# Token-major x and y in a three-stage transformer layer: wide down and output products, roots per token

## The reference

```python
def rmsnorm(x, g):
    y = x * lax.rsqrt(jnp.mean(x * x, axis=-1, keepdims=True) + EPS)
    return y * g
def adaln_in(x, g, shift, scale):
    return rmsnorm(x, g) * (1 + scale) + shift
def swiglu(h, wg, wu, wd):
    return (jax.nn.silu(h @ wg) * (h @ wu)) @ wd
def trunk_layer(x, mod, p, ml_state, ssm_state, n_seg):
    h = adaln_in(x, g[0], sh(0), sh(1))
    x = x + 0.5 * sh(2) * rmsnorm(swiglu(h, p['w_gate'][0], p['w_up'][0], p['w_down'][0]), g[1])
    h = adaln_in(x, g[2], sh(3), sh(4))
    mix, new_ml, new_ssm = hybrid_mixer(h, p, ml_state, ssm_state, n_seg)
    x = x + sh(5) * rmsnorm(mix, g[3])
    h = adaln_in(x, g[4], sh(6), sh(7))
    x = x + 0.5 * sh(8) * rmsnorm(swiglu(h, p['w_gate'][1], p['w_up'][1], p['w_down'][1]), g[5])
```

## Time and profile before

| | us |
|---|---|
| median of 3 executions | 3079.03 |
| lowest and highest of them | 3078.14, 3079.24 |
| the profiled execution, span from first to last instruction | 3079.0 |
| PE busy | 3027.0 (98%) |
| POOL busy | 1825.1 (59%) |
| DVE busy | 1352.3 (44%) |
| ACT busy | 974.9 (32%) |
| mean granted TensorE clock, as a share of full speed | 0.993 |

### The profile page before, as it was taken

One profiled execution on the slowest core, in us unless ns is written; L12 is line 12 of the kernel. 1 busy time (PEld: TensorE's weight loads), 2 busy tenths in 40 slices (PEclk: granted clock), 3 DMA queues, 4 the chain that ended last, 5 costly groups with the idle time before them and its releaser, 6 DMA issues.

```text
span 3079.0 us, 48036 instructions
## 1 busy us (share of the span) xinstructions
PE 3027.0 (98%) x17401; PEld 2859.1 (93%) x17401; DVE 1352.3 (44%) x2931; ACT 974.9 (32%) x1226; POOL 1825.1 (59%) x906
## 2 busy tenths in 40 slices
PE   6999999999999999999999999999999999999998
PEld 2899999999999998899999999899999999999998
DVE  3365566556655665876733352522343111100113
ACT  2322322232222223534332233523222322222223
POOL 2565665566556555557754545566565666566666
PEclk8999999999999999999999999999999999999999
DMA  9866675667566756655444435246554644444443
GB/s 363 280 219 197 220 225 177 206 211 232 175 207 205 232 183 199 220 161 157 138 135 128 118 106 171 73 128 190 168 179 139 143 149 129 126 126 126 126 129 109
DMA packets 494159, 531.54 MB, mean 173 GB/s; under 512 B 29275, under 2 KB 454723, under 8 KB 493123
## 3 DMA queue, kind: packets, MB, share of 16 engines
q1 hardware_dynamic: 458048, 508.62, 52.4%
q10 hardware_dynamic: 35971, 21.27, 2.5%
HBM read 519.12 MB, written 9.66 MB: 172 GB/s over the span
## 4 chain that ended last, share of the span: by engine, by line
PE 91%; DVE 2%; POOL 2%; issue 2%; DMA 1%; ACT 1%; ACTq 1%; DVEq 0%; POOLq 0%
PE banks L784 25%; PE banks L786 25%; PE banks L785 25%; PE banks L959 4%; PE banks L960 4%; PE banks L961 4%; DVE HB L2261 1%; PE banks L870 1%; POOL w_lo L2557 1%; PE banks L813 1%; PE banks L1275 0%; PE banks L1295 0%; DMA w_raw<-in_ffn_w_gate_dram 0%; ACTq L1503 0%; PE banks L1280 0%
## 5 line engine op out<-in xcount | busy, mean ns | idle before, releaser
L2557 POOL TENSOR_TENSOR w_lo<-w_raw,w_hi 128x1024 fp32r<-128x1024 f32 (+1 forms) x668 | 1595.8, 2395 | 1033.0 <-ACT w_hi L1378 1032.5
L784 PE MATMUL banks<-xn_hi,w_hi 128*128 128x384 f32 x3920 | 1329.9, 339 | 5.2 <-POOL w_lo L2557 2.1
L786 PE MATMUL banks<-xn_hi,w_lo 128*128 128x384 f32 x3920 | 1311.7, 335 | 0.0
L785 PE MATMUL banks<-xn_lo,w_hi 128*128 128x384 f32 x3920 | 1311.6, 335 | 0.0
L1378 ACT ACTIVATE w_hi<-w_raw 128x1024 fp32r<-128x1024 f32 (+1 forms) x668 | 704.2, 1057 | 1463.5 <-PE banks L786 743.8
L784 PEld LDWEIGHTS banks<-xn_hi,w_hi 128*128 128x128 f32 x3920 | 737.4, 188 | 29.4 <-issue 22.4
L785 PEld LDWEIGHTS banks<-xn_lo,w_hi 128*128 128x128 f32 x3920 | 737.4, 188 | 4.2 <-issue 3.1
L786 PEld LDWEIGHTS banks<-xn_hi,w_lo 128*128 128x128 f32 x3920 | 736.9, 188 | 0.0
L1876 DVE SCALAR_TENSOR_TENSOR banks<-w_raw,cT,banks 128x256 f32<-128x256 f32 x1372 | 548.0, 483 | 0.0
L1989 DVE TENSOR_TENSOR AM<-AM,banks 128x384 f32<-128x384 f32 x88 | 44.8, 551 | 598.1 <-PE banks L786 598.1
L784 PE MATMUL banks<-hid_hi,w_hi 128*128 128x384 f32 x704 | 235.2, 334 | 0.0
(11 more groups left out here) (293 smaller groups left out, 1819.5 us busy)
## 6 DMA issues: line engine op xcount, KB each, us to landing
w_raw<-in_w_ada_dram SPq DMA_DIRECT2D x288, 512.0 KB, 5.5
w_raw<-in_ffn_w_gate_dram SPq DMA_DIRECT2D x176, 512.0 KB, 4.4
w_raw<-in_ffn_w_up_dram SPq DMA_DIRECT2D x176, 512.0 KB, 3.9
w_raw<-in_ffn_w_down_dram SPq DMA_DIRECT2D x176, 512.0 KB, 3.7
w_raw<-in_w_in_dram SPq DMA_DIRECT2D x104, 512.0 KB, 3.7
w_raw<-in_w_out_dram SPq DMA_DIRECT2D x32, 512.0 KB, 3.5
HB<-row_wait ACTq DMA_DIRECT2D x12, 512.0 KB, 4.7
x_wait<-xT ACTq DMA_DIRECT2D x1, 3072.0 KB, 9.9
```

Of the source, the lines that this page charges most:

```text
L784: pe.matmul(out, wh, hi, start=start, stop=False)
L785: pe.matmul(out, wh, lo, start=False, stop=False)
L786: return pe.matmul(out, w_lo[:, w, off:off + P], hi, start=False, stop=stop)
L2557: pool.tensor_tensor(used(w_lo[:, slot(p), :], p), used(w_raw[:, p % NR, :], p), used(w_hi[:, slot(p), :], p).bitcast(F32), ALU.subtract). ...
```

## The change

- FFN1's down part takes FFN2's form: `wide_piece` with 512 columns, `last_of_ffn` block by block for the last four pieces.
- The output projection is cut into 6 units of 512 columns (two of 6 half parts, two of 2, two of 8) instead of 8 units of 384 tokens by 256 features; a piece has 18 matmuls, the banks go round four, and the last four pieces are walked by groups of 128 tokens (`last_of_out`).
- x lies token-major (`x_tok`) from FFN1's end on. All three stages end with the same `end_of(stage)`: squares with an accumulator on ACT, a root per token, gains on POOL and DVE, `finish`.
- The root of x is put on a diagonal by DVE, spread over all partitions by one matmul with ones for each 128 tokens (`spread_root`) and copied to a row. x is turned back to feature-major by PE: three transposes for each of 16 tiles (`turn`), 4 tiles ahead of use, two banks; `pre_norm` reads them from the banks.
- `coefG` goes to DRAM three times (after FFN1's loop, after the mixer's first products, in FFN2) and is fetched broadcast by SP three times (`load_gains`), each time 2 x 1 MB.
- The first three gate pieces are split among the gains instead of in the tail. WAKE is (0, 6) after FFN1 and (22, 22) after the output projection. The transposes for the output, `keep_x` and the sums by PE are gone.

```diff
-TAIL_ORDER = ((0, 1, 2, 3, 4, 5, 6, 7), (2, 0, 1, 3, 4, 5, 6, 7))
+TAIL_ORDER = (2, 0, 1, 3, 4, 5, 6, 7)
+LAST_BLOCKS = [(c, cc) for c in range(3) for cc in (2, 3)]
+TURN_BANKS = ((1, 4), (4, 6))
+TURN_AHEAD = 4
...
+                    wait_pe(sp, tail_of(n) - 1)
+                    load_gains(2 * n)
+                def load_gains(stage):
+                    sp.wait_ge(g_stored, 32 * (stage + 1))
+                    for g in range(2):
+                        sp.dma_start(g_rows[stage][:, g, :], g_wait[stage, g].partition_broadcast(P)).then_inc(g_loaded, 16)
...
+                def turn(stage, k):
+                    if k >= KT:
+                        return
+                    wait_finished(pe, stage, 2, k // 4)
+                    if k >= 2:
+                        pe.wait_ge(xt_done, KT * (stage + 1) + k - 1)
+                    for c in range(NCH):
+                        last = pe.transpose(psum[TURN_BANKS[stage][k % 2]][:, P * c:P * c + P], x_tok[:, c, P * k:P * k + P], idn[:, :])
+                    last.then_inc(x_turned, 1)
+                def last_of_ffn(n, p0):
+                    for c, cc in LAST_BLOCKS:
+                        wait_added(pe, 2 * n, c, cc - 2)
...
                 ffn(0)
                 pass_pieces(0, NR)
-                for k in range(KT):
-                    square_sum("x1", k)
+                for k in range(2):
+                    turn(0, k)
+                for c in range(2):
+                    spread_root(0, c)
                 pass_pieces(NR, 4 * ADA_PASS)
-                stay_awake(WAKE_PASS)
+                stay_awake(WAKE[0][1])
+                spread_root(0, 2)
+                for k in range(2, TURN_AHEAD):
+                    turn(0, k)
...
+                    for name, c, cc in SQUARES[0][6:]:
+                        square_block(0, name, c, cc)
+                        if (name, c, cc) == ("x", 1, 0):
+                            make_hi(GATE_FIRST[0])
+                        if (name, c, cc) == ("x", 1, 1):
+                            make_hi(GATE_FIRST[1])
+                        if (name, c, cc) == ("x", 2, 0):
+                            make_hi(GATE_FIRST[2])
...
+                    for m, j in enumerate(TAIL_ORDER[:4]):
+                        add_wide(tail_of(n) + m, j, FFN_IT - 1)
+                        if j == 1:
+                            gains_first(2 * n)
+                    end_of(2 * n)
...
+                    pool.wait_ge(g_loaded, 32 * (2 * n + 1))
+                    for c, cc in GAINS[2 * n]:
+                        if n == 0 and (c, cc) == (2, 2):
+                            make_lo(GATE_FIRST[0])
+                            make_lo(GATE_FIRST[1])
+                        gain(2 * n, c, cc)
+                    if n == 0:
+                        make_lo(GATE_FIRST[2])
```

More of the change, by code:

```diff
@@ L189 @@
 MASKED = -1e30
[L190 removed]
+WAKE = ((0, 6), (22, 22))
 STEPS = ((0, 0), (0, 1), (1, 0), (2, 1), (2, 0), (1, 1))
@@ new lines, in turn, with spread_root @@
+                def turn(stage, k):
[7 more added lines that the diff above has]
+                    last.then_inc(x_turned, 1)
+                def spread_root(stage, c):
+                    pe.wait_ge(root_diag, NCH * stage + c + 1)
+                    pe.matmul(ROOT_BANK[:, P * c:P * c + P], ones[:, :], x_dia[:, c, :], start=True, stop=True).then_inc(root_spread, 1)
@@ L1472, in ffn @@
-                    if n == 0:
-                        root(name, D)
+                            store_gains(2)
+                    if n == 0:
+                        store_gains(0)
+                    act.activation(small[:, 0:1], eps[:, 0:1], ACT.Sqrt)
+                    act.activation(warm[:, :], eps[:, 0:1], ACT.Sqrt)
+                    for j in range(5):
+                        split(tail_of(n) + j)
+                        if j == 3:
+                            for c in range(3):
+                                square_block(2 * n, "y", c, 0)
@@ L1518, in _ @@
                 ffn(0)
-                for k in range(KT):
-                    wait_x(act, 0, k)
-                    square("x1", k, xT[:, k, :])
-                root("x1", D)
                 for p, tiles in zip(GATE_FIRST, (range(8), range(8, 12), range(12, 14))):
@@ new lines, in root_bias @@
+                def root_bias(stage, name, c):
+                    for cc in range(3):
+                        wait_squared(dve, stage, name, c, cc)
+                    sums = SUMS[name]
+                    link(dve.scalar_tensor_tensor(out=BIAS[name][:, c:c + 1], in0=sums[:, c, 0:1], scalar=sums[:, c, 1:2],
+                                                  in1=sums[:, c, 2:3], op0=ALU.add, op1=ALU.add))
+                    dve.tensor_scalar(BIAS[name][:, c:c + 1], BIAS[name][:, c:c + 1], 1.0 / D, EPS, ALU.mult, ALU.add).then_inc(
+                        y_biased if name == "y" else x_biased, 1)
@@ L2585, in step @@
                                 split(p, i, per)
-                            if n and part == "first" and (kind, s) == ("g", 1):
+                            if part == "first" and (kind, s) == (("g", 1) if n else ("u", 1)):
                                 if q == 0:
-                                    pool.memset(y_sums[:, :, :], 0.0)
+                                    pool.wait_ge(xt_done, KT)
                                 last = pool.memset(y[:, 4 * q:4 * q + 4, :], 0.0)
```

726 lines of the change are left out of this document (328 added, 398 removed).

## The result

| | before | after |
|---|---|---|
| median, us | 3079.1 | 3109.3 |
| lowest and highest | 3078.1 to 3080.2 | 3107.7 to 3111.0 |
| ratio, 95% interval | | 1.0098, 1.0084 to 1.0112 |
| span of the profiled execution | 3079.0 | 3107.3 |
| mean granted clock | 0.993 | 0.986 |

A forecast was written before the change was run, and what follows sets the result against it. The prediction took PE, busy 98% of the span, as the bound. Its gains and costs summed to +6.5 us on a span of 3079.0, giving 3085.5 us, with a range of 3066 to 3096.

The forecast's parts named there:

- Wide products, FFN1: FFN1's down part: 512-column products take less time than 384-token ones over 11 iterations, -7 us.
- Output projection: Output projection: 576 wide products replace 768, -2.5 us; waits for banks at unit starts, +1 us.
- Gains in the tail: FFN1's tail: DVE waits for stored and fetched gains, idling PE +9.4 us, then a lower clock, +1.7 us.
- rival B: FFN1's tail: the gains store lands in 8 us instead of 17, no stall, total 3074.5 us; chance 0.15.
- End of FFN1: FFN1's end to the gates: late pass pieces delay the first scaled tile, +4 us, and half clock, +1 us.
- rival A: FFN1's end: pass pieces in time, first scaled tile 15 to 17 us after last product, total 3071; chance 0.15.
- Turns among the gates: Gates: transposes of 12 tiles on PE cost +4 us; DVE's scaling is quicker and doesn't hold this up.
- FFN2's first unit: FFN2's first unit: 4 us of turns, less a 1.9 us gap that goes, +2 us.
- Second joint: Output projection to FFN2: first scaled tile 15.5 to 18.5 us after the last product, -9.5 us.
- The store behind the spill: Gates: the second gains store behind the 3 MB spill slows the DMA, +1.5 us (0 to +4).
- Rival D: DVE-POOL locks hold the second joint, first scaled tile at 24, and bank waits come: 3096 us; chance 0.09.
- Rival E: FFN1 and output projection: 512-column products gain nothing over 384, total 3095 us; chance 0.03.

The follow-up runs named there:

- gains_after_adds: The changed kernel with DVE's first gains moved behind the additions of cc=1 in both feed-forward tails: 3104.4 us, ratio to before 1.0083.
- turned_and_three: gains_turned plus the edits of split_earlier, wake_short and pass_first: 3066.3 us, ratio to before 0.9958.
- store_contiguous: The changed kernel with the first gains store written in 64-byte pieces instead of 4, leaving the gains in wrong order: 3096.3 us, ratio to before 1.0061.
- pass_first: The changed kernel with the first eight pass pieces loaded ahead of the gates' first three pieces: 3100.6 us, ratio to before 1.0073.
- spread_before_pass: turned_and_three with FFN1's last root spread after two of the second eight pass pieces, six wake matmuls removed: 3063.1 us, ratio to before 0.9949.
- split_earlier: The changed kernel with second and third weight-piece splits two and four tiles earlier in the gates and FFN2: 3102.3 us, ratio to before 1.0075.
- wake_short: The changed kernel with 2 instead of 22 wake matmuls ahead of the last root spread before FFN2: 3105.2 us, ratio to before 1.0088.
- store_gains_later: The changed kernel with the second gains store moved from behind the spill of x to the mixer's slot 20: 3114.3 us, ratio to before 1.0114.
- gains_turned: The changed kernel with the first two gains stores turned by PE and written in 512-byte pieces, placed later: 3095.0 us, ratio to before 1.0048.

## Why the prediction was wrong

The sign and the mechanism of most steps held. The size did not (6.5 forecast, 30 measured, outside the range), and in the gates and in FFN2's first unit the mechanism was missing (5 and 6). A small part is the measure: the sum was made against a span taken for a time, which it wasn't, by 1.8 us.

1. **Wide products, FFN1** (-7): right, a little over-sized; -5.2 to the tail, and a tail of 32.8 to 33.1 us against 33.6 where nothing waits (gains_after_adds, turned_and_three). An iteration of the loop took 101.97 us before and 101.39 after (from one first down product to the next in PE's timelines), 0.58 less.
2. **Output projection** (-2.5, +1 for banks): -2.8 with the mixer. The bank waits weren't there.
3. **Gains in the tail** (+9.4, +1.7): right, 11.3 and some 2.4 for the restart (46.5 less the gap, against 32.8). store_contiguous shows that the small elements are the cause; rival B (8 us) is excluded. The reason given, that the elements keep all queues busy, is not what this trace shows (see the last section).
4. **End of FFN1** (+4, and +1 for the clock): right, 31.4 against 31 to 32, but for the clock, which was full at the gates; pass_first shows the loads' order as the cause. What stood behind the loads was costed too low: rival A had the first scaled tile at T+15 to T+17 once they were in time, and pass_first has it at 23.6, spread_before_pass at 19.1. But gains_after_adds shows what the text didn't say: steps 3 and 4 share a cause, so the step 3 wait was not there to be had by moving DVE's instruction.
5. **Turns among the gates** (+4, and "don't hold this up"): this is the step that failed. The cost of the transposes was right: where nothing waits and the granted clock is 1.00 (spread_before_pass) the gates take 29.5 us, against 26.8 before with 1.1 of standstill in them, so 3.8. I compared DVE's rate with PE's and found it quicker, and stopped there. But a tile that may be turned only four tiles ahead ties everything behind its scaling to PE's place, and behind it in ACT's and POOL's queues stand the splits of the next weights. That is 3.3 us of gap, and a restart at a clock of 0.65 (1279.48 to 1284.00) that costs 1.6. Of the signs of being wrong that the prediction lists (pass pieces in time, no gap in the tail, PE waiting for banks or for a scaled tile) none came; PE waited for a low part, which isn't among them.
6. **FFN2's first unit** (+2): failed in the same way and more: +10.3. I let the gap of 1.9 us drop out of the sum because two low parts are made earlier than before; the third, which PE needed, stood behind the tiles that wait for the turns. split_earlier took back 7.6 of it.
7. **Second joint** (-9.5): -5.7. The last root was there 15.3 us after the last product, as worked out (15.5 to 18.5 for the first scaled tile). The term had nothing for the 22 wake matmuls that the change puts ahead of the last spread. They stood 5.3 us between the last diagonal and its spread, at a clock of 0.66, and the first scaled tile came at 21.4. In wake_short the joint is 19.8 us, against 24.6 with them and 30.3 before.
8. **The store behind the spill** (+1.5, up to 4): the term was mis-sized, 4.3 us of gap and its restart, 6.0 in all by store_gains_later. I looked at the loads that would be slow; what stood was ACT's own queue, in the issue. Whether the small elements or the place behind the spill make the issue long isn't shown, for the kernels that mended it (gains_turned, turned_and_three) changed both.

The terms missed are 13.7 - 6.5 = 7.2 in the gates, 8.3 in FFN2's first unit, 3.8 in the second joint, 2.7 in the tail: 22.0. The spans' difference (28.3) missed the forecast by 21.8, the small rows cancelling; the medians missed by 23.7, of which some 1.8 is the profiled execution before. Rival D had the second joint (first scaled tile at 24) and bank waits; the first came in part (21.4) and from another cause, the second not at all. Rival E, that 512 columns give nothing over 384, falls: FFN1's loop shortened by 0.58 us an iteration. It was worked out from the start-to-start time that the Trainium skill gives (TensorE: Matmul & The Clock Gate, section "Wait — 56ns, not 53.3ns?"), which these products don't keep.

## What to carry to other kernels

When a producer of tiles is moved onto the engine that consumes them, look past its rate: list what stands behind each tile in the queues of all engines that touch it, for all of that now runs no further ahead than the tile. A small store can be the longest step of a chain; write it in pieces of 64 bytes (store_contiguous) or 512 (gains_turned), also at the cost of a transpose, before looking for a better place for it. And a wake matmul is work on the path as soon as the thing it bridges is shorter than it.

## What the runs showed of the hardware

- Two stores of 2048 elements of 4 bytes, 16 KB together, landed 11.5 and 18.5 us after their issue, with nothing else to carry; the same bytes in pieces of 64 bytes (store_contiguous) landed 1.4 and 1.5 us after theirs. Moving the bytes is less than half of it: the last packet ended 8.1 us after the issue, and for the 9 us ahead of the second landing the trace has no packet at all and no busy DMA. What passes in that time isn't shown. The window (its last two columns are the share of the DMA engines and GB/s):

```profile
1186.50:1195.60 9.10, 8.61 (x38) 6.79 (x37) 1.88 (x3) 3.96 (x8) 5.75 (x3) 1.00 0.00 0
```

- The issue of a DMA can hold up the engine: two issues on ACT's queue took 6.69 us behind a 3 MB store, against 1.37 in the tail, and ACT did nothing else meanwhile.
- A DVE operation of 128x1 took 2.30 us instead of 0.21 (first rows of the second joint). It began 0.5 us into the second of two low parts on POOL, and ended with it at 1968.66 (POOL's timeline):

```profile
1963.53 5.12 POOL L2541 TENSOR_TENSOR w_lo<-w_raw,w_hi 128x1024 fp32r<-128x1024 f32 x2 [6.02 <-ACT w_hi L1370]
```

  The trace agrees with the exclusion of the two engines for a whole instruction that the Trainium skill describes (SBUF — State Buffer, section "SBUF: two separate sides"). So the smallest operation can wait as long as a large one, and this one stood in the chain of the roots.
- Pass pieces at a lower clock: in turned_and_three's joint (PE's timeline) the first eight took 3.63 us at a granted clock of 1.00. The second eight, after PE had stood 7.0 and 2.8 us, took 5.91 at 0.61 (window 1224.20:1230.10):

```profile
1208.12 3.63 PE L834 MATMUL banks<-w_raw,cT 128*2 128x256 f32 x64
...
1224.20 5.91 PE L834 MATMUL banks<-w_raw,cT 128*2 128x256 f32 x64
```
